# Hybrid layer on one core: third block's gate loads moved, masks behind the gating, pooled products in other banks, first merge unit reordered

## The reference

```python
h = rmsnorm(x, norm_g) * (1 + scale) + shift            # scale, shift, gate: silu(c) @ ada_w + ada_b
zs = split_cols(h @ w_in)
gm = gmlp_mix(gelu(u), gelu(v), ln_g, ln_b, w_s, b_s) * silu(gm_g)
na = natten_latent(q, k, v, k_ctx, v_ctx, rpb) * silu(na_g)      # 8 rows x 16 columns around each token, and the context
rw = (norm(y_f + y_b) * gn_g + gn_b + bonus_f + bonus_b) * silu(rw_g)    # y: a recurrence over chunks, both ways
pl = pool_mix(p, w_grp, scale) * silu(pl_g)
x = x + gate * (sum_i sigmoid(merge_i) * (branch_i @ w_br[i])) @ w_out
out = rmsnorm(x, final_g)
```

## Time and profile before

| | us |
|---|---|
| median of 3 runs (2515.11 to 2519.92) | 2515.48 |
| the profiled execution | 2524.0 |
| its span in the trace | 2522.3 |
| chain stage in the trace | 1845 to 1971 |
| attention stage | 1971 to 2155 |
| merge stage | 2155 to 2522 |
| TensorE busy in the chain stage, and its granted clock | 102.5 of 126, 0.84 |

### The profile page before, as it was taken

How to read it: one execution, slowest core, us unless ns; L and a number is a source line. 1 busy time by engine, 2 the same in 40 slices (tenths; PEclk the granted TensorE clock), 3 DMA queues, 4 the chain that set the end, 5 groups by cost and what they waited for, 6 DMA issues and landing times. The chain is left out here.

```text
span 2522.3 us, 65173 instructions
## 1 busy us (share of the span) xinstructions
PE 2259.8 (90%) x26434; PEld 1847.0 (73%) x26434; DVE 1569.3 (62%) x2604; ACT 1011.2 (40%) x1734; POOL 192.0 (8%) x256
## 2 busy tenths in 40 slices
PE   4999999999899999999947787787879798899998
PEld 2788878888688887888836666666757576678887
DVE  5755656666865456666556666666546677756754
ACT  5444234445432124444335544444423665312111
POOL 0000000000000000000040100000014560000000
PEclk8999999999999999999969999999979899999999
DMA  6344333333333332333221111110048623735542
GB/s 234 110 136 121 104 100 121 100 112 121 105 99 96 106 104 93 110 121 100 96 70 35 35 54 39 35 35 20 21 166 300 161 73 100 259 128 179 200 142 92
DMA packets 250411, 279.50 MB, mean 111 GB/s; under 512 B 30682, under 2 KB 174170, under 8 KB 247642
## 3 DMA queue, kind: packets, MB, share of 16 engines
q1 hardware_dynamic: 245130, 266.82, 32.9%
q10 hardware_dynamic: 4752, 8.53, 0.9%
q0 software_dynamic: 320, 0.98, 0.2%
HBM read 184.66 MB, written 91.62 MB: 110 GB/s over the span
## 5 line engine op out<-in xcount | busy, mean ns | idle before, releaser
L715 PE MATMUL proj_ps<-h_hi,w_hi 128*128 128x512 f32 x1656 | 649.6, 392 | 28.2 <-DVE h_lo L465 19.9
L716 PE MATMUL proj_ps<-h_lo,w_hi 128*128 128x512 f32 x1656 | 647.1, 391 | 0.0
L717 PE MATMUL proj_ps<-h_hi,w_lo 128*128 128x512 f32 x1656 | 646.8, 391 | 0.0
L318 ACT CAST w_hi<-w_raw 128x512 fp32r<-128x512 f32 x420 | 255.1, 621 | 695.1 <-PE proj_ps L717 353.0
L715 PEld LDWEIGHTS proj_ps<-h_hi,w_hi 128*128 128x128 f32 x1656 | 312.6, 189 | 98.2 <-issue 26.6
L717 PEld LDWEIGHTS proj_ps<-h_hi,w_lo 128*128 128x128 f32 x1656 | 312.3, 189 | 65.7
L716 PEld LDWEIGHTS proj_ps<-h_lo,w_hi 128*128 128x128 f32 x1656 | 312.6, 189 | 63.5
L482 DVE TENSOR_TENSOR w_lo<-w_raw,w_hi 128x512 fp32r<-128x512 f32 x420 | 283.1, 688 | 44.3 <-ACT w_hi L318 43.8
L498 DVE TENSOR_TENSOR z_slots<-proj_ps,x_rows 128x512 f32<-128x512 f32 x174 | 120.2, 691 | 170.1 <-PE proj_ps L717 168.0
L498 DVE TENSOR_TENSOR x_rows<-proj_ps,x_rows 128x512 f32<-128x512 f32 x116 | 80.1, 691 | 109.7 <-PE proj_ps L717 103.7
L1140 DVE TENSOR_TENSOR inv_g<-rw_ps,level_masks 128x512 f32<-128x512 f32 x90 | 62.0, 689 | 100.5 <-PE rw_ps L1308 100.3
(11 more groups left out here) (366 smaller groups left out, 4012.4 us busy)
## 6 DMA issues: line engine op xcount, KB each, us to landing
w_raw<-in_w_in SPq DMA_DIRECT2D x240, 256.0 KB, 3.0
scratch_gatesT<-z_slots SPq DMA_DIRECT2D x128, 256.0 KB, 2.7
late_rows<-scratch_gatesT SPq DMA_DIRECT2D x64, 512.0 KB, 4.3
scratch_zT<-z_slots SPq DMA_DIRECT2D x108, 256.0 KB, 2.5
ada<-in_ada_w SPq DMA_DIRECT2D x4, 2048.0 KB, 15.5
late_rows<-scratch_zT SPq DMA_DIRECT2D x4, 2048.0 KB, 12.5
late_rows<-scratch_branchT SPq DMA_DIRECT2D x16, 512.0 KB, 4.9
late_rows<-in_x SPq DMA_DIRECT2D x16, 512.0 KB, 4.5
```

Of the source, the lines that this page charges most:

```text
L318: A.copy(wh[:, i, :, :], raw[:, q, :, :]).then_inc(w_hi, 1)
L715: T.matmul(out, wh[:, i, k, :], hi[:, o, k, :], start=(first and k == 0), stop=False, skip_group_check=not first)
L716: T.matmul(out, wh[:, i, k, :], lo[:, o, k, :], start=False, stop=False, skip_group_check=not first)
L717: last = T.matmul(out, wl[:, i, k, :], hi[:, o, k, :], start=False, stop=(k == 3), skip_group_check=not first)
```

## The change

Five edits.

1. The nine small loads of parameters (`gm_ln_g` and the others, 4-byte or 512-byte runs) are issued by SyncE behind `load_ada(0)`, ahead of the second block's loads, where ScalarE issued them ahead of its first gelu.
2. Block 2's bonus and gate go into `gt[:, 0]`, the buffer of block 0's g rows, which is free once `outputs(0, 1)` is done. `load_gates(2)` stands right behind that, ahead of y of block 2; q comes behind y of block 2, and v behind y of block 3. Each block has a semaphore of its own for these loads. ScalarE's `gates(2)` moves ahead of `squares(2)`, VectorE's `gated_bonus(2)` ahead of `summed(3, 0)`, and `gated_values(2)` ahead of `finished(1)`.
3. `mask_bias` moves from ahead of block 3's `roots` to behind block 3's `ug`.
4. The pooled products go to banks 0, 2, 4 and 0 (`POOLED`), so blocks 1 and 2 wait for nothing, and block 3 for block 0's gating, which VectorE now does in the turn of grid row 30.
5. The first merge unit takes its twelve matmuls by product: high times high, then the low weights, then the low rows, with a wait ahead of each.

The core of the diff:

```diff
-        bonus_of = lambda b: late_part(s["late"], L_BONUS, BLK) if b == NB - 1 else gin[:, b % 2, 4:6, :]
-        gate_of = lambda b: late_part(s["late"], L_RG, BLK) if b == NB - 1 else rg[:, b % 2]
+        bonus_of = lambda b: late_part(s["late"], L_BONUS, BLK) if b == NB - 1 else gt[:, 0, 0] if b == 2 else gin[:, b, 4:6, :]
+        gate_of = lambda b: late_part(s["late"], L_RG, BLK) if b == NB - 1 else gt[:, 0, 1] if b == 2 else rg[:, b]
...
             load_ada(0)
+            for n, name in enumerate(("gm_ln_g", "gm_ln_b")):
+                sp.dma_start(lnp[:, n, :], t[name].rearrange("l (m h) n -> (h n) (l m)", h=2)).then_inc(bias_in, 16)
+            for g in range(4):
+                sp.dma_start(bs[half(g % 2), g // 2, :], t["gm_bs"][0, g:g + 1, :].to_broadcast([CH, P])).then_inc(bias_in, 16)
+            sp.dma_start(ada_bias[:], t["ada_b"].rearrange("l (m p) -> p (l m)", p=P)[:, 2 * KT:3 * KT]).then_inc(ada_b_in, 16)
...
             sp.wait_ge(s_done, 4 * (STEPS + 1))
+            o_p.after(sp, 0, "o1")
+            load_gates(2)
+            load_y(2)
             sp.dma_start(late_part(s["late"], L_Q, SEQ), z(T_Q, slice(Z_LAT, Z_LAT + SEQ))).then_inc(s["na_in"]["q"], 16)
-            load_y(2)
             gm_v.after(sp, 3, "m1")
             store(0, 3, 3)
+            load_y(3)
             load_na(T_V, L_V, "v")
-            load_y(3)
             rw_v.after(sp, 0, "out")
-            load_gates(2)
             store(4, 0, NB)
...
-                if b == NB - 1:
-                    mask_bias()
...
+            mask_bias()
             for b in range(NB - 1):
                 roots(rw_g, b, lambda: rw_x.after(pool, b, "seed"), (nx[:, b % 2], ny[:, b % 2]))
...
             spread_roots(0)
+            gates(2)
             squares(2)
             spread_roots(1)
-            squares(3, (0,))
-            gates(2)
-            squares(3, (1,))
+            squares(3)
...
             summed(2, 1)
+            gated_bonus(2)
             summed(3, 0)
             statistics(2)
             summed(3, 1)
+            gated_values(2)
             finished(1)
-            gated_values(2)
-            gated_bonus(2)
             statistics(3)
...
+        POOLED = (0, 2, 4, 0)
...
+                    if r == ROWS - 2:
+                        pooled(0)
...
-            for b in range(NB):
-                dve.wait_ge(pl_silu, b + 1)
+            for b in range(1, NB):
+                pooled(b)
...
-                if b >= 2:
-                    pe.wait_ge(pl_out, b - 1)
+                if b == NB - 1:
+                    pe.wait_ge(pl_out, 1)
                 for p in range(2):
-                    last = T.matmul(ps[:, 2 * (b % 2) + p, :], plw[:, p, :], dd[:, p, b * BLK:(b + 1) * BLK], start=True, stop=True)
+                    last = T.matmul(ps[:, POOLED[b] + p, :], plw[:, p, :], dd[:, p, b * BLK:(b + 1) * BLK], start=True, stop=True)
...
+                if (n, i, p) == (0, 0, 0):
+
+                    parts = [(c, k) for c in range(2) for k in range(2)]
+                    col = lambda c: slice(c * P, (c + 1) * P)
+                    pe.wait_ge(w_h, 1)
+                    pe.wait_ge(b_h, 1)
+                    for c, k in parts:
+                        T.matmul(ps[:, 0, c, :], w_hi[:, 0, k, col(c)], b_hi[0][:, k, :], start=(k == 0), stop=False)
+                    pe.wait_ge(w_l, 1)
+                    for c, k in parts:
+                        T.matmul(ps[:, 0, c, :], w_lo[0][:, k, col(c)], b_hi[0][:, k, :], start=False, stop=False)
+                    pe.wait_ge(b_l, 1)
+                    for c, k in parts:
+                        last = T.matmul(ps[:, 0, c, :], w_hi[:, 0, k, col(c)], b_lo[:, 0, k, :], start=False, stop=(k == 1))
```

More of the change, by code:

```diff
@@ L1672, in load_gates @@
                 lat = slice(CTX + b * BLK, CTX + (b + 1) * BLK)
[L1673 to L1675 removed]
+                sp.dma_start(bonus_of(b), t["bonusT"][:, :, lat].rearrange("m p t -> p m t")).then_inc(b_in[b], 16)
+                sp.dma_start(gate_of(b), z(T_RG, cols(b))).then_inc(b_in[b], 16)
             def load_ada(n):
@@ L1940, in gelus @@
                 gelu(b, "u", 0, ug_in[b % 2], 32 * (b // 2 + 1))
[L1943 to L1947, removed]
-            act.dma_start(gn[:, 0, :], t["rw_gn_g"].rearrange("l (m p) -> p (l m)", p=P)).then_inc(gn_in, 16)
-            act.dma_start(gn[:, 1, :], t["rw_gn_b"].rearrange("l (m p) -> p (l m)", p=P)).then_inc(gn_in, 16)
             gelu(0, "v", 2, v_in[0], 16)
@@ L1972, in gates, with squares @@
                     rw_in_a.done(A.activation(bonus, bonus, ACT.Identity, bias=gn[:, 1, p:p + 1]), f"bonus{p}")
-            def squares(b, pairs=(0, 1)):
-                for p in pairs:
+            def squares(b):
+                for p in range(2):
                     rw_o.after(act, b, f"o{p}")
@@ L2418, in v_copy, with pooled @@
                 V.tensor_copy(value_rows(n), turned_values(n)).then_inc(v_copied[1], 1)
+            def pooled(b):
+                if b == 0:
+                    dve.wait_ge(plw_in, 16 * 5)
+                dve.wait_ge(pl_silu, b + 1)
+                dve.wait_ge(pl_ps, b + 1)
+                for p in range(2):
+                    gate = pg[:, p, b * BLK:(b + 1) * BLK]
+                    last = V.scalar_tensor_tensor(gate, ps[:, POOLED[b] + p, :], pls[:, p:p + 1], gate, ALU.mult, ALU.mult)
+                last.then_inc(pl_out, 1)
             dve.wait_ge(wins_zero, 1)
@@ L2458, in _ @@
                     V.tensor_tensor(rows, rows, q[:, 0, 0:D], ALU.mult).then_inc(scaled, 1)
-            dve.wait_ge(plw_in, 16 * 5)
-            for b in range(NB):
-                dve.wait_ge(pl_silu, b + 1)
-                dve.wait_ge(pl_ps, b + 1)
-                for p in range(2):
-                    gate = pg[:, p, b * BLK:(b + 1) * BLK]
-                    last = V.scalar_tensor_tensor(gate, ps[:, 2 * (b % 2) + p, :], pls[:, p:p + 1], gate, ALU.mult, ALU.mult)
-                last.then_inc(pl_out, 1)
+            for b in range(1, NB):
+                pooled(b)
         @block.tensor
@@ L2794, in unit @@
             def unit(n, i, p):
+                if (n, i, p) == (0, 0, 0):
[11 more added lines that the diff above has]
+                        last = T.matmul(ps[:, 0, c, :], w_hi[:, 0, k, col(c)], b_lo[:, 0, k, :], start=False, stop=(k == 1))
+                    last.then_inc(units, 1)
+                    return
                 if n == 0 and p % 2 == 0:
```

11 lines of the change are left out of this document (5 added, 6 removed).

## The result

The changed kernel takes 2508.56 us (median of 20 runs, 2502.04 to 2519.89), the kernel before 2521.96 us beside it (20 runs, 2515.11 to 2528.14). The ratio is 0.995, with 95% interval 0.9939 to 0.9962: 12.5 us faster (9.6 to 15.4); the medians themselves lie 13.4 us apart. The forecast was 2500.5 us with a range of 2496 to 2508, so the sign is right and the time lies 0.56 us above the range. The profiled execution has a span of 2512.7 us and a granted clock of 0.965.

A forecast was written before the change was run, and what follows sets the result against it. TensorE, busy for 90% of the span, bounds the kernel; its waits and those at stage ends can be won. Terms 6.3 + 5.6 + 1.7 + 1.4 = 15.0 us, from 2515.5 to 2500.5 us, range 2496 to 2508.

The forecast's parts named there:

- The text's other figure, 2509.0: Whole kernel: the profiled execution of 2524.0 us less the forecast gain of 15.0 us.
- The sum: Whole kernel: gains of 6.3 + 5.6 + 1.7 + 1.4 = 15.0 us.
- Small loads, 6.3: Chain stage's start: without nine loads on ScalarE the first gelu ends at 1851.7 and TensorE starts sooner; 6.3 us.
- the second rival: Chain stage's start: small loads on SyncE hold back block 1; first term falls to 2.5 us, 2504.3 in all; 15 in 100.
- no load waited for the one before it: Slower case: each small load lands only after the previous one, v near 1905, kernel 2538 us; 3 in 100.
- The first rival: Chain stage's start: the pause is ScalarE waiting for instructions; gain 2.2 us instead of 6.3, 2504.6 in all; 15 in 100.
- Masks, 2.4 and 1.1 for the clock: Chain stage's middle: block 3's roots come sooner, 2.4 us; TensorE's idle nearly goes and block 0's products run faster, 1.1 us.
- Block 2's gate, 2.1: Chain stage's tail: VectorE loses 0.95 us of waiting for the late gate and 1.14 us of work; 2.1 us.
- Pooled products, 1.7: Attention's end: TensorE no longer waits for a bank before the last pooled products; 1.7 us, ends 1 and 1.8.
- First unit, 1.4: Merge's start: TensorE starts when the high rows are made, not both low parts; 1.4 us.
- the case for which the text had 0.5: Merge's start: the first unit gains only 0.5 us if the rise of TensorE's clock stays where it is.

The follow-up runs named there:

- e12: The kernel before, unaltered, profiled and timed again: ratio 1.0002, median 2526.04 us.
- e8: The changed kernel, unaltered, profiled and timed again against the kernel before: ratio 0.9936.
- e4: The kernel before with only the banks of the pooled products and the order of the first merge unit changed: ratio 0.9994.
- e6: The changed kernel with the nine small loads on SyncE behind block 1's v, u and gate instead of ahead: ratio 0.9941 to the kernel before.
- e1: The kernel before with only the nine small loads moved from ScalarE to SyncE: ratio 0.9972, 7.1 us faster.
- e2: The kernel before with only the masks moved behind block 3's product of u and gate: ratio 0.9979, 5.3 us faster.
- e3: The kernel before with only block 2's gate loads, SyncE's transfer order and the operations moved for it: ratio 0.9992.
- e7: The changed kernel without its second edit (block 2's gate, transfer order and operations as before): ratio 0.9943 to the kernel before.
- e11: The changed kernel without its second edit and with v issued behind k: ratio 0.9959 to the kernel before.
- e9: The changed kernel with v issued behind k instead of behind y of block 3: ratio 0.9959 to the kernel before.

## Why the prediction came out as it did

**What failed: the base.** "It lies 8.5 us above the median of the runs shown; the changed stretches have nothing that scales with that, so the difference is taken from the median." The three runs shown, 2515.48 in the median, are the first three of the twenty and were low ones, by chance as far as the runs tell (the changed kernel's first three are not low). The kernel before has 2521.96 over 20 runs, 2524.55 to 2525.97 in the three later comparisons and 2526.04 in e12; the profiled execution's 2524.0 was its ordinary time. From the median of the 20 runs the same 15.0 us lead to 2507.0. So of the 8.1 us between forecast and measured time, 6.5 are the base and 1.6 the sum. The text's other figure, 2509.0 from the profiled execution, comes still nearer to 2508.56, but there two errors offset each other: a base 2.0 us high and a sum that is too large. In the fourteen profiles the chain stage starts between 1837.9 and 1849.9, after code that is the same in all: 12 us of scatter ahead of everything that was changed. A median over three of such runs is no base to 1 us, and a range of 12 us had little room for it.

**The sum.** 15.0 us forecast; 12.5 (9.6 to 15.4) and, in e8, 16.2 (12.4 to 19.7) measured. By the profiles (changed and e8 against before, e12 and for the chain e4, means) the last product of the chain comes 9.9 us sooner (11.9 forecast), the attention's end is 1.2 us shorter (1.7), the merge 1.1 us (1.4): 12.2 us. So the 15.0 us lie inside both intervals of the timings, while the profiles put the gain nearer to 12.

**Small loads, 6.3.** Right: 6.7 us at `gate(0, 0)`, 7.1 us (4.0 to 9.9) timed alone. The first gelu came 4.42 us into the stage, where 1851 was 5.8 us into it. Block 1 was not held back in a way that lasts (e6, e8), so the second rival falls, and no load waited for the one before it.

The first rival is wrong in its time and not in its mechanism. It had the gelu late even without the small loads, and the gelu came with v (e1). But it named the pause as ScalarE's wait for its instructions while the transfers are saturated, and the traces speak for that. In all five profiles with these loads on ScalarE (before, e2, e3, e4, e12) a packet of 8 KB in queue 14, the other instruction queue, starts 1.61 to 1.65 us before ScalarE goes on, while the transfer engines are busy for 0.9 to 1.07 of each us ahead of it. This is its row in the first profile of before, in the window from 1852.75 to 1853.00, ahead of the load at 1854.58:

```profile
q14 instruction: 1, 0.01, 7.7%
```

SyncE's slow issues among the same loads (1.47 and 2.77 us) look different: there the issue itself is long, where ScalarE's issues of these two took 0.48 and 0.38 us. No run has the nine loads on ScalarE in another order, which would part its place in the program from the load ahead of the pause, so this stays a reading of the packets.

**Masks, 2.4 and 1.1 for the clock.** Right in size: no idle ahead of the products, 3.95 us for them; 3.4 to 4.8 us in e2's profile, 5.3 (2.8 to 8.1) timed. What the text did not have is the pause in block 1 that comes with it, 0.79 to 1.77 us.

**Block 2's gate, 2.1.** Mis-sized: "So the 3.5 us (2.4 + 1.1) goes through to the sum of block 3, and the tail behind that loses 0.95 of waiting and 1.14 of work." The tail did lose 2.2 us against the first profile, but 0.95 us of that wait was one execution's. And the 3.5 us did not go through whole. In block 1 the masks' edit brings a pause (e2, e7), whether this edit's loads are there or not. In blocks 2 and 3 this edit's loads, issued sooner, lie where TensorE's next instructions are due: 0.37 to 1.84 us of pauses there in the seven profiles with the edit, at most 0.19 in the seven without. By e7 and by e11 the edit is worth nothing. The trace of before had the mark of such pauses, 0.36 us of "issue" before the same five products; the prediction did not read it.

**Pooled products, 1.7.** 1.2 us, in every profile with the edit; between the text's ends of 1 and 1.8.

**First unit, 1.4.** Its first matmul is 1.46 us sooner as forecast, and the merge 1.1 us shorter by the means, 0.7 by the first two profiles. TensorE is at its lower level for all twelve matmuls (granted clock 0.50 from 2148 to 2152, 0.54 from 2152 to 2154), the case for which the text had 0.5.

**What stays open.** How much the instruction pauses cost in time, since their removal could not be had without the late stores; a v issued ahead of k, but later than right behind y of block 3, was not tried. Nor was a cause found for the 5.2 to 8.6 us between rows 0 and 1. The clock has a part: it averages 0.59 to 0.63 in the four profiles with 7.7 to 8.6 us (changed, e4, e6, e7). But it is 1.00 in five others (e3, e8 to e11), and they take 6.5 to 7.0 us, with 1.8 to 2.7 us of TensorE's wait for ScalarE's `probs_t`, where the 5.2 us of before have 0.40 of it. These are rows of the changed kernel, then of e12:

```profile
1988.00:1990.00 2.00, 1.70 (x32) 1.70 (x34) 1.27 (x4) 2.00 (x5) 1.92 (x2) 0.50 0.83 280
1990.00:1992.00 2.00, 2.00 (x27) 1.88 (x24) 0.80 (x5) 0.09 (x1) 1.92 (x2) 0.50 0.04 7
```

```profile
1996.00:1998.00 2.00, 2.00 (x50) 1.93 (x49) 1.93 (x7) 1.68 (x4) 1.92 (x2) 0.78 0.36 79
1998.00:2000.00 2.00, 2.00 (x21) 1.56 (x24) 0.93 (x4) 1.50 (x3) 2.00 (x1) 1.00 0.00 0
```

## What to carry to other kernels

Take the base of a forecast from where the time scatters least and from all that is known of it: when three runs and a profiled execution lie 8.5 us apart, the base is between them, and the range is at least that wide. A transfer that is moved forward is not free because its reader is later: it lies in the queues with the program's own instructions and with stores that a stage's end waits for, and it can cost there what it saves. A wait that one profile shows once is a price only after a second profile shows it again. And an idle time that ends with "issue" in the middle of a run of equal instructions is worth a look at the instruction queues.

## What the runs showed of the hardware

TensorE stops for 0.3 to 1.8 us at fixed places of its program, 126 matmuls, as many weight loads and four semaphore instructions apart, at times when large transfers fill the queues. A packet of 16 KB in an instruction queue starts 2.2 to 2.6 us before it goes on. Full queues alone don't make a pause: in e12, e1 and e4 the transfer engines are busy for 0.89 to 1.06 of the 4 us ahead of each place, and no pause is over 0.1 us. What parts the cases is how early the packet starts, and where it started 2.8 us or more ahead, TensorE never paused. With the queues half free (e9, block 3) the packet came 3.95 us ahead and the place passed without a pause. ScalarE stops for 5.0 to 5.3 us in five profiles, and an 8 KB packet in the other instruction queue starts 1.6 us before it goes on; that this is the same wait was not tested.

The Trainium skill, "Runtime: NRT & Kernel Launch", Instruction fetch mechanics, says that instructions come in blocks of 256 through the engine's own transfers and that crossing into the next is mostly hidden. The distance of 126 + 126 + 4 instructions agrees with that; "mostly hidden" doesn't hold here while the queues are full.
